# Norm sums in a one-core hybrid block: squares summed on VectorE, raw tiles one at a time, condition rows and the root's table earlier

## What is computed

```python
def rms_norm(x, g, eps=NORM_EPS):
    xf = x.astype(jnp.float32)
    y = xf * lax.rsqrt(jnp.mean(xf * xf, axis=-1, keepdims=True) + eps)
    return (y * g.astype(jnp.float32)).astype(x.dtype)

def swiglu(h, w_gate, w_up, w_down):
    return (jax.nn.silu(h @ w_gate) * (h @ w_up)) @ w_down

# block 2: six vectors of silu(c) @ w + b, with c one row of 1024
def ada(cvec, w, b):
    return jnp.split(jax.nn.silu(cvec) @ w + b, 6, axis=-1)
```

## Time and profile before

| | us |
|---|---|
| median of 3 runs | 3945.76 (3933.8 to 3946.42) |
| the profiled execution | 3944.55 |
| span of its trace (first to last instruction) | 3942.8 |
| PE busy | 3700.4 (94%) |
| DVE busy | 1566.9 (40%) |
| ACT busy | 1234.4 (31%) |
| POOL busy | 1232.8 (31%) |

### The profile page before, as it was taken

The page is one execution under the profiler, slowest core; times in us unless marked ns, Lnnn a source line. Parts: engine busy times, 40 slices in busy tenths (PEclk is TensorE's granted clock), DMA queues, the critical chain, the costliest instruction groups (busy, mean ns, idle before and its releaser), DMA issues.

```text
span 3942.8 us, 47689 instructions
## 1 busy us (share of the span) xinstructions
PE 3700.4 (94%) x17904; PEld 3047.9 (77%) x17904; DVE 1566.9 (40%) x2656; ACT 1234.4 (31%) x1840; POOL 1232.8 (31%) x516
## 2 busy tenths in 40 slices
PE   8999997689999999999768999989989999989999
PEld 7888776687888788877558788877768888778887
DVE  4430585744330433049565533122453321223220
ACT  3222435223222322243533322222323332323331
POOL 3444330003444344433000344423101444323443
PEclk9999996799999999999669999989999999999999
DMA  4442220003442344222000244322101222212222
GB/s 170 145 143 91 75 81 1 1 12 110 146 144 95 118 144 144 91 71 80 11 1 1 86 145 147 107 75 70 44 6 43 86 98 98 70 54 80 97 99 92
DMA packets 93535, 332.10 MB, mean 84 GB/s; under 512 B 10432, under 2 KB 12128, under 8 KB 93280
## 3 DMA queue, kind: packets, MB, share of 16 engines
q1 hardware_dynamic: 77136, 274.65, 19.9%
q10 hardware_dynamic: 16272, 55.65, 4.0%
HBM read 327.64 MB, written 2.62 MB: 84 GB/s over the span
## 4 chain that ended last, share of the span: by engine, by line
PE 88%; DVE 7%; ACT 2%; DMA 2%; issue 1%; SPq 0%; ACTq 0%; DVEq 0%
PE ps L1757 22%; PE ps L1758 22%; PE ps L1759 22%; PE ps L1791 2%; DMA w_raw<-in_tiles 1%; PE ps L1901 1%; PE ps L2499 1%; PE ps L1776 1%; PE ps L1781 1%; PE ps L2053 1%; PE ps L1777 1%; PE ps L2484 1%; PE ps L1894 1%; PE ps L2232 1%; PE ps L1821 1%
## 5 line engine op out<-in xcount | busy, mean ns | idle before, releaser
L446 POOL TENSOR_TENSOR w_lo<-w_raw,w_hi 128x1024 fp32r<-128x1024 f32 x512 | 1232.6, 2409 | 2686.5 <-ACT w_hi L468 2686.3
L1757 PE MATMUL ps<-h_hi,w_hi 128*128 128x512 f32 x2656 | 1049.9, 395 | 22.6 <-DVE sil L1106 13.6
L1759 PE MATMUL ps<-h_hi,w_lo 128*128 128x512 f32 x2656 | 1037.9, 391 | 0.0
L1758 PE MATMUL ps<-h_lo,w_hi 128*128 128x512 f32 x2656 | 1037.6, 391 | 0.0
L468 ACT ACTIVATE w_hi<-w_raw 128x1024 fp32r<-128x1024 f32 x512 | 541.4, 1058 | 1137.9 <-DMA w_raw<-in_tiles 1137.7
L1757 PEld LDWEIGHTS ps<-h_hi,w_hi 128*128 128x128 f32 x2656 | 501.3, 189 | 143.5 <-issue 29.2
L1758 PEld LDWEIGHTS ps<-h_lo,w_hi 128*128 128x128 f32 x2656 | 501.4, 189 | 105.5 <-issue 3.4
L1759 PEld LDWEIGHTS ps<-h_hi,w_lo 128*128 128x128 f32 x2656 | 500.9, 189 | 106.0
L1111 DVE TENSOR_TENSOR a_lo<-sil,a_hi 128x512 f32 (+1 forms) x132 | 299.4, 2268 | 479.5 <-ACT a_hi L585 479.5
L1757 PE MATMUL ps<-a_hi,w_hi 128*128 (+1 forms) x1056 | 415.8, 394 | 0.0
L1758 PE MATMUL ps<-a_lo,w_hi 128*128 (+1 forms) x1056 | 414.6, 393 | 0.0
(11 more groups left out here) (444 smaller groups left out, 4031.8 us busy)
## 6 DMA issues: line engine op xcount, KB each, us to landing
w_raw<-in_tiles SPq DMA_DIRECT2D x512, 512.0 KB, 3.2
ada_raw<-in_ada_tiles ACTq DMA_DIRECT2D x96, 512.0 KB, 3.2
x<-in_x_t SPq DMA_DIRECT2D x2, 1024.0 KB, 6.4
sq<-in_cond ACTq DMA_DIRECT2D x4, 512.0 KB, 4.1
out_t<-x SPq DMA_DIRECT2D x1, 2048.0 KB, 7.1
consts<-in_consts SPq DMA_DIRECT2D x1, 1280.0 KB, 12.7
mem<-in_ctx_t ACTq DMA_DIRECT2D x1, 1024.0 KB, 7.6
core_mem<-in_consts ACTq DMA_DIRECT2D x1, 576.0 KB, 3.7
```

The lines of the kernel that those rows point to most:

```text
L446: nc.gpsimd.tensor_tensor(w_lo[:, s, :], w_raw[:, s, :], w_hi[:, s, :].bitcast(F32), ALU.subtract).then_inc(S["w_lo_ready"], 1)
L1757: nc.tensor.matmul(bank, wh, hi, start=first, stop=False, skip_group_check=True)
L1758: nc.tensor.matmul(bank, wh, lo, start=False, stop=False, skip_group_check=True)
L1759: return nc.tensor.matmul(bank, wl, hi, start=False, stop=last, skip_group_check=True)
```

## The change

Four things at once.

1. **Sums.** Square 0 goes into `sq[:, 0, :]` (`square_sum`), squares 1 to 7 into three slots in turn. DVE adds squares 1 to 6 to `square_sum` (`add_square`, L1091 of the changed kernel), and PE sums only `square_sum` and square 7 (`sum_squares`): 8 calls per norm for 32. None is left between the tiles of a down or an out projection.
2. **Raw pair.** `raw_tiles` does the first tile over all chunks, then the second. In it the sums come after chunk 3 (after an FFN) or 1 (after an out projection), the spread two chunks later. After an FFN the pair uses banks 4 and 5, else 0 and 1. `raw_used`, which frees a raw chunk for its normed one, is signalled in the second tile. DVE normalises straight from `ps[:, 7, :]` and copies the root to `mem` last.
3. **Condition rows.** In FFN 1, 2 and 3 the loads are issued ahead of the normed chunks, and the row's `Silu` comes behind that of the first activation.
4. **Root's table.** A one-element `Sqrt` (`load_sqrt`) ahead of the squares loads the table.

```diff
+            def load_sqrt():
+                nc.scalar.activation(rtok[:, 0:1], eps(EPS_ONE), ACT.Sqrt)
...
             def norm_raw(name, updates):
-                for n in range(seen.pop("early"), KD):
+                for n in range(early, KD):
                     square_x(n, order[n], updates)
-                for k in todo[:len(todo) // 2]:
-                    raise_raw(name, k)
-                act.wait_ge(S["ss_ready"], seen["sq_slot"])
+                    if early + 2 == KD:
+                        raise_raw(name, todo[n - early])
+                if early + 2 < KD:
+                    for k in todo:
+                        raise_raw(name, k)
+                act.wait_ge(S["ss_ready"], due("norms"))
                 nc.scalar.activation(rtok[:, :], ps[:, 7, 0:TB], ACT.Sqrt, scale=1.0 / D, bias=eps(EPS_NORM)).then_inc(S["std_ready"], 1)
...
+                if name.startswith("ffn") and int(name[-1]) < 4:
+                    load_cond(int(name[-1]))
                 for n, k in enumerate(order):
...
-                    if n in (4, 6):
-                        round_tile(base + 4 + (n - 4) // 2)
+                    if n in (4, KD - 1):
+                        round_tile(base + 4 + n // (KD - 1))
...
+            def add_square(n):
+                if n == 0:
+                    return
+                dve.wait_ge(S["sq_ready"], KD * seen.get("std_ready", 0) + n + 1)
+                if n > 1:
+                    dve.wait_ge(S["sq_added"], due("sq_added"))
+                else:
+                    due("sq_added", int("sq_added" in seen))
+                nc.vector.tensor_tensor(square_sum, square_sum, square_slot(n), ALU.add).then_inc(S["sq_added"], 1)
...
                         nc.vector.scalar_tensor_tensor(x[:, k, :], ps[:, k, :], gate(k), x[:, k, :], ALU.mult, ALU.add).then_inc(S["x_ready"], 1)
+                        if half == 0 and d and n < 2 * DEPTH + 1:
+                            add_square(d + 3)
...
                     V.tensor_tensor(x[:, k, :], x[:, k, :], ps[:, (k - 1) % KD, :], ALU.add).then_inc(S["x_ready"], 1)
+                    add_square(max(k - 1, 0))
                     if 0 < k < KD - 1:
                         lower_raw(RAW_NEXT[f"mix_out{l}"], k - 1)
...
+            def sum_squares():
+                norms = due("norms")
+                for last, chunk in enumerate((square_sum, square_slot(KD - 1))):
+                    if last:
+                        pe.wait_ge(S["sq_ready"], KD * norms)
+                    else:
+                        pe.wait_ge(S["sq_added"], (KD - 2) * norms)
+                    for j in range(TB):
+                        ins = nc.tensor.matmul(ps[:, 7, j:j + 1], chunk[:, j * P:(j + 1) * P], const("ones", 0, 1), ...)
+                ins.then_inc(S["ss_ready"], 1)
...
-                    if half == 0 and n < 2 * DEPTH + 1:
-                        for c in range(KD // 2):
-                            sum_chunk(c)
...
-                    if k >= 3:
-                        sum_chunk(k - 3)
```

More of the change, by code:

```diff
@@ L475, in square_x @@
                     act.wait_ge(x_loaded[k // (KD // 2)], 16)
-                if due("sq_slot") > len(squares):
-                    act.wait_ge(S["ss_ready"], seen["sq_slot"] - len(squares))
-                nc.scalar.activation(squares[n % len(squares)], x[:, k, :], ACT.Square).then_inc(S["sq_ready"], 1)
+                norms = seen.get("norms", 0)
+                if n == 0 and norms:
+                    act.wait_ge(S["ss_ready"], norms)
+                if n > len(squares):
+                    act.wait_ge(S["sq_added"], (KD - 2) * norms + n - len(squares))
+                nc.scalar.activation(square_slot(n), x[:, k, :], ACT.Square).then_inc(S["sq_ready"], 1)
+            def load_sqrt():
+                nc.scalar.activation(rtok[:, 0:1], eps(EPS_ONE), ACT.Sqrt)
             def raise_raw(name, k):
@@ L548, in load_ada, with load_cond, silu_cond @@
                 act.dma_start(ada_raw[:, q % 2, :], io["ada_tiles"][q]).then_inc(ada_loaded[q % 2], 16)
+            def load_cond(n):
+                for c, row in enumerate(cond_rows(n)):
+                    act.dma_start(row, io["cond"][c].partition_broadcast(P)).then_inc(S["cond_loaded"], 16)
+                    due("cond_loaded", 16)
+                load_ada(ADA_PER_FFN * n)
+            def silu_cond(n):
+                act.wait_ge(S["cond_loaded"], seen["cond_loaded"])
+                for row in cond_rows(n):
+                    nc.scalar.activation(row, row, ACT.Silu).then_inc(S["cond_ready"], 1)
             def ffn(n, order, updates, shift=None):
@@ L556, in ffn @@
                     norm_x(order, updates, shift=shift)
-                if n < 4:
-                    for c, row in enumerate(cond_rows(n)):
-                        act.dma_start(row, io["cond"][c].partition_broadcast(P)).then_inc(S["cond_loaded"], 16)
-                        loaded = due("cond_loaded", 16)
-                    load_ada(ADA_PER_FFN * n)
-                    act.wait_ge(S["cond_loaded"], loaded)
-                    for row in cond_rows(n):
-                        nc.scalar.activation(row, row, ACT.Silu).then_inc(S["cond_ready"], 1)
+                if n < 4 and not raw:
+                    load_cond(n)
+                    silu_cond(n)
                 def pairs(i):
@@ L643, in attention @@
                     act.wait_ge(S["w_used"], base + m + 1)
-                    nc.scalar.activation(mem[:, att_unit(m), :], ps[:, 4 + m if m < 2 else m % 2, :], ACT.Copy).then_inc(S["proj_out"], 1)
+                    nc.scalar.activation(mem[:, att_unit(m), :], ps[:, raw_banks(f"att_in{l}")[m] if m < 2 else m % 2, :], ACT.Copy).then_inc(S["proj_out"], 1)
                     if m >= 2:
@@ L1140, in ffn @@
                         nc.vector.scalar_tensor_tensor(x[:, k, :], ps[:, k, :], gate(k), x[:, k, :], ALU.mult, ALU.add).then_inc(S["x_ready"], 1)
+                        if half == 0 and d and n < 2 * DEPTH + 1:
+                            add_square(d + 3)
+                    if half and n < 2 * DEPTH + 1:
+                        for d in range(KD // 2):
+                            add_square(d)
                     if half and after:
@@ L1783, in first_tiles, with norm_sums @@
                             ins.then_inc(S["w_used"], 1)
-            def sum_chunk(n):
-                pe.wait_ge(S["sq_ready"], due("sq_ready"))
-                for j in range(TB):
-                    ins = nc.tensor.matmul(ps[:, 7, j:j + 1], squares[n % len(squares)][:, j * P:(j + 1) * P], const("ones", 0, 1),
-                                           start=(n == 0 and j == 0), stop=(n == KD - 1), skip_group_check=True)
-                ins.then_inc(S["ss_ready"], 1)
-                seen["early"] = n + 1
-            def sum_squares():
-                for n in range(seen.get("early", 0), KD):
-                    sum_chunk(n)
-                seen["early"] = 0
+            def sum_squares():
[6 more added lines that the diff above has]
+                    for j in range(TB):
+                        ins = nc.tensor.matmul(ps[:, 7, j:j + 1], chunk[:, j * P:(j + 1) * P], const("ones", 0, 1),
+                                               start=(last == 0 and j == 0), stop=(last == 1), skip_group_check=True)
+                ins.then_inc(S["ss_ready"], 1)
+            def norm_sums():
+                sum_squares()
                 spread_rstd()
```

88 lines of the change are left out of this document (50 added, 38 removed).

## The result

The changed kernel takes 3884.68 us (median of 4 runs, 3880.47 to 3888.65), the kernel before 3939.78 (4 runs: the three of the table above and a fourth of 3929.6): ratio 0.9862 with a 95% interval of 0.9832 to 0.9892, or 55.1 us between the medians. Forecast were 53.1 us and 3892.5; of the 7.8 us between 3892.5 and 3884.68, 6.0 are the fourth run, which moved the median before from 3945.76 to 3939.78.

The account below looks back on a forecast made before the run. PE was taken to bound the kernel, 88% of the span. Gains of 30.8, 14.6, 13.8 and 7.6 less 0.4, 9.0, 3.8 and 0.5 gave 53.1 us, hence 3892.5, range 3880 to 3905 (8 in 10: 3866 to 3912).

Parts of the forecast that it names:

- Middle of the FFNs: Down projections of FFN 0 to 4: removing PE's mid-FFN sums gains 5.2 us in two, 6.8 in three, +30.8.
- Between the out tiles: Four out projections: removing four chunks of sums each between tiles gains 16 x 0.91, +14.6 us.
- `ffn1` and `ffn3`: Crossings into these FFNs with a raw pair: 17.2 us before, 10.3 after, +13.8 for both.
- the wait for `sil` that comes of the condition row's DMA: Crossings into `ffn1` and `ffn3`: PE's 4.56 us wait comes from this DMA and goes with the earlier row.
- After a raw crossing's wait: Crossings with a raw pair: 1.70 us of sums, 1.05 for the spread, 3.4 of lower clock follow PE's idle time.
- `att_in0` and `att_in1`: Crossings with a raw pair into these stages: 8.8 us before, 9.0 after, -0.4 for both.
- `mla_in` and `fourier_in`: Crossings after FFN 3 and 4 without a raw pair: root at 8.3 us for 3.76, -9.0 for both.
- `ffn4` and `ffn5`: Crossings after `mla_out` and `fourier_out` without a raw pair: root at 6.8 us for 4.9, -3.8 for both.
- Rival 1: At the crossings POOL does not hold the adds, so waits and slow stretches shrink: gain 72 us, 3873; chance 0.16.
- Rival 2: Crossings cost more, with longer waits in half the norms and longer half clock in six: gain 33, 3913; chance 0.14.
- Rival 3: The weight stream takes back PE's freed time, ACT waiting for DMA with PE behind it: 3942; chance 0.04.
- rival 4: Slower: each of three adds at a crossing meets POOL anew, 8.2 us per crossing, 74 in all: 3966; chance 0.04.

Follow-up runs that it names:

- experiment 4: Changed kernel plus 16 or 8 extra sum calls in the middle of FFN 0 to 4: 45.7 and 27.8 us with a wait for squares, 27.7 and 9.0 without.
- experiment 5: Changed kernel with condition rows loaded behind the normed chunks again: 0.85, 0.98 and 1.26 us more in `ffn1`, `ffn2`, `ffn3`; whole execution 3895.88 us.
- experiment 6: Changed kernel with the raw pair done chunk by chunk again: 4.5, 5.7 and 5.1 us more in `ffn1`, `ffn2`, `ffn3`; -1.4 and +1.0 in the `att_in`.
- Experiment 1: Changed kernel with ACT's last weight-tile rounding at each crossing moved behind the root: 3857.41 us, 0.9806 of the kernel before; crossings 33.9 us less.
- experiment 7: Changed kernel with a one-element `Silu` added ahead of the wait for `raw_scaled`: 0.8, 2.2 and 0.9 us less in `ffn1`, `ffn2`, `ffn3`, 3.8 together.

## Why the prediction was right, and where it was not

**The sum.** 53.1 us forecast, 55.1 between the medians, 56.9 by the places. Term by term:
- *Middle of the FFNs*: +30.8, measured 30.9, and nothing took its place; experiment 4 put the price back. DVE and ACT had the cover named.
- *Between the out tiles*: +14.6, measured 15.2. Four calls cost the whole 0.95 us of their row; I had taken an overlap off.
- *The program's start*: -0.5, measured -0.9, less than the 1.6 us by which kernels with the same code there differ.
- *`ffn1` and `ffn3`*: +13.8, measured 13.7. The size was right by luck, the cause was not. The step "the wait for `sil` that comes of the condition row's DMA" failed. I took the DMA from the chain and put the whole 4.56 us of the wait on it. Undone alone in the changed kernel, the early row is worth 1.0 us an FFN (experiment 5) and the tile-wise pair 5.1 (experiment 6). Before, DVE was itself late: the `h_lo` and `sil` rows of 2.48 and 2.77 were part of the chain that ended in that wait, just ahead of the DMA. I had read them as a price of POOL and not followed them to PE.
- *After a raw crossing's wait* I had 1.70 for the sums, 1.05 for the spread and 3.4 for a slow stretch of products: 6.15. Measured in `ffn1` are 3.05, 1.54 and 1.5, in `att_in0` 3.34, 1.25 and 1.5, both 6.1. The sum holds because two errors cancel: I let the clock fall behind the sums, and it was low in them. For the crossings without a raw pair I had the sums at half clock, rightly.
- *`ffn2`*: +7.6, measured 9.0. PE's wait was 1.7 and not 2.2, and its sums, 1.95 us there, kept the full clock.
- *`att_in0` and `att_in1`*: -0.4, measured +2.0. I had taken `att_in1` at the price of `att_in0`; before, it cost 1.5 us more (12.3 and 10.8), and in the changed kernel both cost 10.6. The wait was 1.84 for 2.2.
- *`mla_in` and `fourier_in`*: -9.0, measured -7.1. In `mla_in` PE waited 4.40 us and the root came 3.61 behind the first sum, 8.0 together for 8.3: 4.1 lost. I had charged both places alike, but `fourier_in`, whose root came later before, lost 3.0 only.
- *`ffn4` and `ffn5`*: -3.8, measured -5.9. The mechanism was right (wait 3.21 ahead of the sums) and the size off: the lower clock also lasts longer behind the norm. Here are the stretches in which the first normed products run, from 2.5 us (before) and 1.5 us (after) behind the first of them, with the clock third from the end:

```profile
3061.00:3065.00 4.00, 4.00 (x17) 3.20 (x17) 3.89 (x7) 2.17 (x3) 0.00 (x0) 0.93 0.01 4
```

```profile
2998.00:3001.50 3.50, 3.50 (x10) 2.73 (x9) 3.42 (x5) 2.06 (x3) 0.00 (x0) 0.50 0.00 0
```

**The new wait.** Three things were right: that a two-operand add in SBUF would be held by POOL, that it would be the first one at an FFN's end, and how long PE would stand: rows 7 gave 2.48 to 2.77 us, the add took 2.48; 2.2 and 2.85 us of idle were forecast, 1.84 and 2.46 were measured. Experiment 1 shows that it is POOL that holds the add.

**The rivals.** Rival 1 (adds not held) didn't happen. It describes the kernel of experiment 1, and there I had priced it too low: 19 us over the forecast, 33.9 measured. Its sum doesn't follow its own words: they say 2 us in each of nine norms and the slow stretch of 3.4 in half of them, which is 33; the sum has 9 x 1 and 3 x 3.4. (Its reading of rows 6 is off as well: ACT's squares start 0.17 us ahead of POOL, not behind.) The edit gave 5.2 us in each `att_in`, 2.8 in `ffn2`, 4.1 in `ffn1` and `ffn3`, 5.0 in `mla_in` and 2.8 in `ffn4` and `ffn5`. Rival 2 had the `ffn4` and `ffn5` part of its mechanism, 2 us in all. Rival 3, the weight stream, did not decide anywhere: though every tile is wanted sooner, no tile of a down projection is waited for. In rival 4 the adds were to meet POOL anew each time. At the end of an out projection one add does, the fifth square's (2.47 us ahead of `ffn1`), and that was already in my 2.85; the price stayed far from the 5.9 us per crossing at which it would have decided.

**The `Silu` load.** 1.3 us was forecast in series with PE's wait, and 1.26 was measured, without a drain (experiment 7).

**The root's table.** Part 4 of the change has no experiment of its own. I counted nothing for it, and the trace before bears that out. ACT at the start of `att_in0` there:

```profile
396.05 1.28 ACT L494 ACT_TABLE_LOAD   x1
...
399.88 0.27 ACT L494 ACTIVATE rtok<-ps,consts 128x4 f32<-128x4 f32 x1 [2.55 <-PE ps L1791]
```

Behind the load ACT was idle for 2.55 us until PE's sums came, so the load was not on the path; in rows 12 it idled 0.91 and 1.99 us at this point.

## What to carry to other kernels

Work taken off the bounding engine gains its own time and the clock that it cost, but look where its replacement stands last: the adds were free in 40 us of cover, and POOL's hold on one of them cost 34 us at nine places where the next step needed it at once. Before you move work to DVE, look what POOL runs there and whether the operation reads two operands from SBUF; if so, move POOL's instruction, or what releases it, to the far side of the critical step. And when a wait is put down to the last thing that ended, undo that thing alone before believing its price: here the DMA named was worth 1.0 us, beside a wait of 4.6.

## What the runs showed that I had not expected

- The price of sums goes up faster than their number. Eight calls in the middle of an FFN cost 1.80 us at all five places with the granted clock at 1.00. Sixteen cost 5.2 to 6.8.
- A run on untouched code varies more than this change's smaller parts. Mixer 0 takes 294.8 to 303.5 us beyond its products and mixer 1 293.2 to 303.6, in kernels whose code is the same there, and not both high or low together. The granted clock over mixer 1 was 0.79 in the profile before, 0.81 in the one after. What sets it stays open. A comparison place by place leaves the mixers out, though a single place still varies by up to 2.4 us; a difference of two single executions holds all of it: the profiles differ by 64 us, the medians by 55.
- Tile order mattered more through the ring of weight slots than through PE. The first slot free one tile, 5.2 us, sooner was worth 5.1 us an FFN by the table, 2.3 of them in PE's wait ahead of the fifth tile.
